# Attention of the samples in a decoder step: keys turned by VectorE in 32x32 blocks, scores in sixteen array tiles, their partial sums added by products with stacked identities

## What is computed

```python
def one(args):
    ql, qp, cn, kn, pages = args
    cp = cache_ckv[pages].reshape(-1, KV_LORA)
    kp = cache_kpe[pages].reshape(-1, QK_ROPE_DIM)
    n_past = cp.shape[0]
    s_past = (jnp.einsum('thl,pl->htp', ql, cp) + jnp.einsum('thr,pr->htp', qp, kp)).astype(jnp.float32) * ATTN_SCALE
    s_new = (jnp.einsum('thl,sl->hts', ql, cn) + jnp.einsum('thr,sr->hts', qp, kn)).astype(jnp.float32) * ATTN_SCALE
    s_new = jnp.where(causal, s_new, -jnp.inf)
    p = jax.nn.softmax(jnp.concatenate([s_past, s_new], axis=-1), axis=-1).astype(cp.dtype)
    return jnp.einsum('htp,pl->thl', p[..., :n_past], cp) + jnp.einsum('hts,sl->thl', p[..., n_past:], cn)
```

## Time and profile before

| | before |
|---|---|
| median of 3 executions | 1428.21 us |
| profiled execution, its own time | 1430.2 us |
| profiled execution, its span | 1428.1 us |
| TensorE (PE) busy | 1373.9 us, 96% |
| VectorE (DVE) busy | 829.4 us, 58% |
| ScalarE (ACT) busy | 612.6 us, 43% |
| GpSimd (POOL) busy | 728.0 us, 51% |
| bytes moved | 148.67 MB, of which the gathers 41.95 MB |

### The profile page before, as it was taken

The page is one execution under the profiler, slowest core; times in us unless marked ns, Lnnn a source line. Parts: engine busy times, 40 slices in busy tenths (PEclk is TensorE's granted clock), DMA queues, the critical chain, the costliest instruction groups (busy, mean ns, idle before and its releaser), DMA issues.

```text
span 1428.1 us, 28640 instructions
## 1 busy us (share of the span) xinstructions
PE 1373.9 (96%) x12250; PEld 1274.6 (89%) x12250; DVE 829.4 (58%) x1247; ACT 612.6 (43%) x1044; POOL 728.0 (51%) x505
## 2 busy tenths in 40 slices
PE   6999989999999999999999988889999999999997
PEld 6778679999999999999999856566999999999997
DVE  6768865755464553767566645555475554645434
ACT  5222354644344343444666533343364443444432
POOL 3333113388788786443323533330346787887831
PEclk9999989999999999999999999999999999999998
DMA  9221202223322224432111576661122223222221
GB/s 226 61 57 35 92 0 90 89 91 103 103 90 89 90 90 139 148 99 65 34 34 53 198 270 252 253 228 41 60 89 89 89 92 112 94 89 89 89 89 63
DMA packets 123181, 148.67 MB, mean 104 GB/s; under 512 B 13552, under 2 KB 114160, under 8 KB 118832
## 3 DMA queue, kind: packets, MB, share of 16 engines
q1 hardware_dynamic: 115888, 104.90, 23.4%
q0 software_dynamic: 7168, 41.95, 7.8%
HBM read 142.81 MB, written 4.03 MB: 103 GB/s over the span
## 4 chain that ended last, share of the span: by engine, by line
PE 93%; DVE 4%; ACT 2%; issue 1%; DMA 0%; POOL 0%; DVEq 0%; SPq 0%; ACTq 0%
PE ps L1609 33%; PE ps L1756 20%; PE ps L1744 18%; PE ps L1888 6%; PE ps L1652 4%; PE ps L1928 3%; PE ps L1980 2%; ACT wh L678 1%; PE ps L1661 1%; PE ps L1673 1%; PE ps L1971 1%; PE ps L1989 0%; PE ps L1713 0%; PE ps L1833 0%; DVE kt L1447 0%
## 5 line engine op out<-in xcount | busy, mean ns | idle before, releaser
L541 POOL TENSOR_TENSOR wl<-raw,wh 128x512 fp32r<-128x512 f32 (+2 forms) x252 | 439.9, 1748 | 443.2 <-ACT wh L678 443.0
L678 ACT ACTIVATE wh<-raw 128x512 fp32r<-128x512 f32 (+2 forms) x253 | 192.6, 762 | 376.1 <-PE ps L1609 205.9
L541 POOL TENSOR_TENSOR wl<-wuv,wh 128x512 fp32r<-128x512 f32 x104 | 135.3, 1312 | 78.1 <-ACT wh L678 78.1
L1609 PE MATMUL ps<-xh,wh 128*128 128x272 f32 x704 | 149.9, 294 | 14.0 <-DVE xl L1033 13.3
L1756 PE MATMUL ps<-mh,wl 128*128 128x272 f32 x768 | 158.6, 288 | 0.0
L1756 PE MATMUL ps<-mh,wh 128*128 128x272 f32 x768 | 158.6, 288 | 0.0
L1756 PE MATMUL ps<-ml,wh 128*128 128x272 f32 x768 | 158.3, 288 | 0.0
L1609 PE MATMUL ps<-xh,wl 128*128 128x272 f32 x704 | 146.3, 290 | 0.0
L1609 PE MATMUL ps<-xl,wh 128*128 128x272 f32 x704 | 146.0, 289 | 0.0
L1609 PEld LDWEIGHTS ps<-xh,wh 128*128 128x128 f32 x704 | 111.4, 191 | 25.2 <-POOL wl L541 11.5
L1756 PEld LDWEIGHTS ps<-ml,wh 128*128 128x128 f32 x768 | 120.4, 188 | 0.0
(11 more groups left out here) (316 smaller groups left out, 3052.7 us busy)
## 6 DMA issues: line engine op xcount, KB each, us to landing
raw<-w_up SPq DMA_DIRECT2D x32, 1024.0 KB, 5.2
raw<-w_down SPq DMA_DIRECT2D x32, 1024.0 KB, 5.0
raw<-w_pw SPq DMA_DIRECT2D x16, 512.0 KB, 5.1
raw<-w_pw SPq DMA_DIRECT2D x4, 1024.0 KB, 6.7
raw<-w_o SPq DMA_DIRECT2D x4, 1024.0 KB, 5.8
raw<-w_dq SPq DMA_DIRECT2D x3, 1024.0 KB, 5.3
raw<-w_uq SPq DMA_DIRECT2D x4, 768.0 KB, 4.4
x<-xT SPq DMA_DIRECT2D x4, 544.0 KB, 7.4
```

Of the source, the lines that this page charges most:

```text
L541: pf.tensor_tensor(weight(wl, u), weight_raw(u), f32(weight(wh, u)), ALU.subtract).then_inc(w_lo, 1)
L678: af.activation(weight(wh, u), weight_raw(u), ACT.Copy).then_inc(w_hi, 1)
L1609: m = tf.matmul(ps[:, bank_of(u) + bank, 0:width], w[:, k, :], a[:, k, part], start=(k == 0 and n == 0), stop=(k == nk - 1 and n == 2))
```

## The change

- VectorE turns the keys itself, from the gathered rows in SBUF to SBUF, with its own transpose (`df.transpose`), which turns each 32x32 block in place: `keys(i, c)` has two transposes of 1024 columns for c = 0 and 1 (the two halves of the latent) into `k_far`, and two of 512 columns for c = 2 (the rotary part) into `k_rot`. The 40 turns on TensorE and the ten copies to `kt` fall away, and `kt` and `ORDER` with them.
- The blocks so turned leave the numbers of one key only in the 32 partitions of its own block. So the scores become products of 32 rows by 32 queries: each of the array's sixteen 32x32 tiles works alone (`scores_s`). The four row tiles r write their own PSUM banks (`RING[r]`), each for the keys whose block lies in these partitions; the four column tiles g hold partial sums over different 32 numbers of the key. For c = 0 and 1 there are 16 products of 512 columns, for c = 2 there are 8.
- ScalarE copies the four banks to `kq` (`quarters_out`), and 16 products of 128 columns with `ident4`, four 32x32 identities stacked on each other, add the four partial sums (`quarters`). They write the bank in which the scores stood before. The columns of the scores now come in another order, which the access pattern of the exponentials and the choice of rows in `values` undo.
- The queries are first brought to the partitions that this needs, once: five pairs of products (`queries_turned`), copied by ScalarE and VectorE into `raw` and `acc`.
- `k_far`, `k_rot` and `kq` have one buffer each. `keys(i + 1, c)` waits until `scores_s(i, c)` is done (`k_used`).
- `kq` and the queries lie in `raw`, so all loads of `w_o` behind the first wait until the last scores are added.
- Copies of outputs and the collecting (`values_out`, `collect`) move from VectorE to ScalarE. `folds` moves to POOL, between gathers, but for the last. `weights` is split in `differences` and `weights`.
- On TensorE the scores for c = 0 and 1 of the next piece stand where the turns stood; those for c = 2 stand before `values`.

The diff, cut to its core:

```diff
         r_in = [sem(f"r_in{i}") for i in range(CB)]
-        kt_mm, kt_act, kt_dve = sem("kt_mm"), sem("kt_act"), sem("kt_dve")
+        q_mm, q_act, q_dve = sem("q_mm"), sem("q_act"), sem("q_dve")
...
         RSTD = ps[:, 4:6, :].rearrange("p a b -> p (a b)")[:, 0:T]
-        def keys_at(n):
-            return ps[:, RING[n % 4], :]
...
+        def q_of(j):
+            return q_near[:, j, :] if j < DC else q_rot[:, j - DC, :]
+
+        def k_of(j):
+            return k_far[:, j // 4, :, SB * (j % 4):SB * (j % 4 + 1)] if j < DC else k_rot[:, :, SB * (j - DC):SB * (j - DC + 1)]
...
             for n in range(units[U_WO].block, len(blocks)):
+                if n == units[U_WO].block + 1:
+                    sp.wait_ge(ks_mm, NSC)
                 load(n)
...
+            def folds(b):
+                pool.wait_ge(e_wn, b + 1)
+                if b >= SETS:
+                    pool.wait_ge(e_mm, 1)
+                for s in range(SETS):
+                    pf.tensor_tensor(fold_w[NS * s:NS * (s + 1), b % SETS, :, :], ident32.unsqueeze(1).to_broadcast([NS, SPB, NS]),
+                                     wn[:, s, :].unsqueeze(2).to_broadcast([NS, SPB, NS]), ALU.mult).then_inc(e_fold, 1)
+                g = b % SETS
+                pf.tensor_scalar(fold_new[NS * g:NS * (g + 1), g, :], ident32, wn[:, SETS, 0:1], None, ALU.mult).then_inc(e_fold, 1)
+
...
             for j in range(4, NCH):
                 gather(j)
+                if j > CB and (j - CB) % (2 * SPB) == 3:
+                    folds((j - CB) // (2 * SPB))
+            folds(NB - 2)
...
+            def queries_turned(p):
+                act.wait_ge(q_mm, p + 1)
+                af.activation(q_pair(p).rearrange("p j q -> p (j q)"), q_bank(p), ACT.Copy).then_inc(q_act, 1)
...
-                    keys(0, (0, 2))
+                    act.wait_ge(w_lo, PROJ[NH - 1] + 1)
+                    queries_turned(0)
+                    queries_turned(2)
...
+            def quarters_out(i):
+                act.wait_ge(k_used, 3 * (i + 1))
+                if i > 0:
+                    act.wait_ge(ks_mm, i)
+                for g in range(GROUPS):
+                    af.activation(kq[:, g, :], ps[:, RING[g], :], ACT.Copy).then_inc(kq_out, 1)
+
+            def values_out(i):
+                act.wait_ge(ko_mm, i + 2)
+                if i >= SETS * SPB:
+                    act.wait_ge(e_mm, 1)
+                af.activation(oc_at(i), ps[:, 6, 0:KL], ACT.Copy).then_inc(ko_out, 1)
...
+            def collect(b):
...
-            keys(0, (8,))
+            act.wait_ge(w_lo, U_WO + 2)
             for i in range(NSC):
-                keys(i + 1, (0,))
+                quarters_out(i)
+                if i == 0:
...
+                if i == FOLD_AT + 1:
+                    turned_out(0)
+                if i > 0 and i != FOLD_AT:
+                    values_out(i - 1)
+                if i % SPB == 0 and i > 0:
+                    weights_out(i // SPB - 1)
                 act.wait_ge(ks_max, i + 1)
-                af.activation(ss[:, :], ps[:, 3 + i % 2, :], ACT.Exp, bias=nmx[:, i % SETS:i % SETS + 1], scale=SCALE,
-                              accum_out=st[:, i % SETS, 1:2]).then_inc(ks_exp, 1)
+                af.activation(ss[:, :].rearrange("p (g i s) -> p i g s", g=SETS, i=GROUPS),
+                              ps[:, 3 + i % 2, :].rearrange("p (i g s) -> p i g s", i=GROUPS, g=SETS), ACT.Exp,
+                              bias=nmx[:, i % SETS:i % SETS + 1], scale=SCALE, accum_out=st[:, i % SETS, 1:2]).then_inc(ks_exp, 1)
                 if i == FOLD_AT:
+                    values_out(i - 1)
                     folded_out(0)
-                keys(i + 1, (2, 4, 6))
+                if i % SPB == SPB - 1:
+                    collect(i // SPB)
                 probs_out(i)
-                if i == FOLD_AT:
-                    turned_out(0)
-                keys(i + 1, (8,))
-                if i % SPB == SPB - 1:
-                    weights_out(i // SPB)
+            weights_out(NB - 1)
+            values_out(NSC - 1)
...
+            def keys(i, c, halves_=(0, 1)):
+
                 if i >= NSC:
                     return
-                for g in groups:
-                    dve.wait_ge(kt_mm, 10 * i + g + 1)
-                    df.tensor_copy(kt[:, ORDER[g], :], keys_at(10 * i + g)).then_inc(kt_dve, 1)
+                if i > 0:
+                    dve.wait_ge(k_used, 3 * (i - 1) + c + 1)
+                for g in halves_:
+                    j = 2 * i + g
+                    if c == 0:
+                        dve.wait_ge(c_in[j % CB], 16 * (j // CB + 1))
+                    if c == 2:
+                        dve.wait_ge(r_in[j % CB], 16 * (j // CB + 1))
+                    to, a = ((k_rot[:, RPC * g:RPC * (g + 1), :], rotaries(j).rearrange("p (r l) -> p r l", r=RPC)) if c == 2 else
+                             (k_far[:, c, RPC * g:RPC * (g + 1), :],
+                              latents(j).rearrange("p (r l) -> p r l", r=RPC)[:, :, c * P:(c + 1) * P]))
+                    df.transpose(to, a).then_inc(k_turned, 1)
...
-            def collect(b):
...
-            def weights(b):
+            def differences(b):
...
+            def weights(b):
...
-            keys(0, (3, 5, 7, 9))
+            keys(0, 0, (1,))
+            queries_turned(3)
+            keys(0, 1)
+            keys(0, 2)
             for i in range(NSC):
-                if i > 0 and i != FOLD_AT:
-                    values_out(i - 1)
+                keys(i + 1, 0)
+                keys(i + 1, 1)
+                if i % SPB == 0 and i > 0:
+                    weights(i // SPB - 1)
                 dve.wait_ge(ks_mm, i + 1)
                 m = st[:, i % SETS, 0:1]
                 link(df.tensor_reduce(m, ps[:, 3 + i % 2, :], AX.X, ALU.max))
                 df.tensor_scalar(nmx[:, i % SETS:i % SETS + 1], m, -SCALE, None, ALU.mult).then_inc(ks_max, 1)
-                if i == 0:
-                    dve.wait_ge(ko_mm, 1)
-                    df.tensor_copy(onew[:, :, :].rearrange("p a b -> p (a b)"), ps[:, 6, :]).then_inc(ko_out, 1)
-                if i == FOLD_AT:
-                    values_out(i - 1)
-                keys(i + 1, (1, 3, 5, 7, 9))
+                keys(i + 1, 2)
                 if i % SPB == SPB - 1:
-                    collect(i // SPB)
-                    weights(i // SPB)
-                elif i > 0:
-                    folds(i // SPB - 1)
+                    differences(i // SPB)
+            weights(NB - 1)
             folds(NB - 1)
-            values_out(NSC - 1)
...
-            def keys(i, groups):
...
-                    for q in range(4):
-                        a = (rotaries(j)[:, 2 * q * ROPE:2 * (q + 1) * ROPE] if k == 4 else
-                             latents(j)[:, (2 * q + k // 2) * KL + (k % 2) * P:(2 * q + k // 2) * KL + (k % 2 + 1) * P])
-                        m = tf.transpose(keys_at(n)[:, q * P:(q + 1) * P], a, ident)
-                    m.then_inc(kt_mm, 1)
+            def queries_turned(p):
+
+                for n in range(2):
+                    j = 2 * p + n
+                    row = SB * (j % 4)
+                    for r in range(GROUPS):
+                        m = tf.matmul(q_bank(p)[SB * r:SB * (r + 1), n * NB * NS:(n + 1) * NB * NS], ident[:, row:row + SB],
+                                      qs[:, j // 4, :, :].rearrange("p b q -> p (b q)"), start=True, stop=True)
+                m.then_inc(q_mm, 1)
...
@@ -1915,19 +1964,31 @@
                     if h // 2 + 1 < NH // 2:
                         values_product(h // 2 + 1, h % 2)
                 else:
-                    keys(0, range(3))
+                    pe.wait_ge(kcopy, 2 + 4 * NH // 2 + KC)
+                    for p in range(3):
+                        queries_turned(p)
                 outputs(h)
 
             def scores_s(i, c):
+
                 b = i // SPB
-                pe.wait_ge(kt_act, 5 * i + (4, 5, 5)[c])
-                pe.wait_ge(kt_dve, 5 * i + (3, 4, 5)[c])
-                for s in range(SETS):
-                    q = qs[:, c if c < KC else KC + s % 2, b, :]
-                    k = kt[:, 5 * (s // 2) + (2 * (s % 2) + c if c < KC else 4), :]
-                    m = tf.matmul(ps[NS * s:NS * (s + 1), 3 + i % 2, :], q, k, start=(c == 0), stop=(c == 2))
-                if c == 2:
-                    m.then_inc(ks_mm, 1)
+                pe.wait_ge(k_turned, 6 * i + 2 * c + 2)
+                for r in range(GROUPS):
+                    part = slice(SB * r, SB * (r + 1))
+                    for g in range(GROUPS if c < 2 else 2):
+                        j = 4 * c + g
+                        m = tf.matmul(ps[SB * g:SB * (g + 1), RING[r], :], q_of(j)[part, b * NS:(b + 1) * NS], k_of(j)[part, :, :],
+                                      start=(c == 0), stop=(c == (2 if g < 2 else 1)))
+                m.then_inc(k_used, 1)
+
+            def quarters(i):
+
+                for r in range(GROUPS):
```

(39 more changed lines are left out.)

69 lines of the change are left out of this document (31 added, 38 removed).

## The result

The changed kernel is slower, by 1.9%: 1457.95 us median of 4 (1453.6 to 1459.61), beside 1429.2 (1428.06 to 1432.48) of the kernel before; ratio 1.0193, 95% interval 1.0164 to 1.0221. The forecast was 1387 us. The profiled execution took 1453.6 us, with a span of 1451.8. The first maximum of the loop starts at 833.77 us (forecast 828.0), the last at 1012.38 (947.0): the loop takes 178.6 us instead of 119.0, and this is where nearly all of the miss lies. Behind it nothing changed (439.4 us of span against 440.7 before).

What follows compares the result with a forecast made beforehand. VectorE was to bound the changed loop at 8.05 us a piece instead of 10.95; -40.4 us to the last maximum and -0.6 behind took 1430.2 to 1389.2 profiled, the median 2.0 lower: 1387 us, range 1380 to 1396.

Steps and rivals of the forecast that it cites:

- the price of the scores: TensorE in each piece: 80 score instructions at 34 ns, the convolution's pace, 2.7 us.
- The gathers: Cache loads per piece: POOL issues in 5.0 us, data take 6.9 us, fitting in 8.05 with slack 1.5.
- the head: Before the loop: the first maximum waits for VectorE alone and starts at 828.0 us instead of 825.0.
- the sum: VectorE's work per piece in the loop: 0.98 + 6.14 + 0.93 = 8.05 us, where a piece took 10.95.
- rival 1: Loop: gathers or TensorE bound it, VectorE being quicker; 7.3 us a piece, 1376 us; chance 0.12.
- The gain: Whole program: -40.4 us to the last maximum and -0.6 behind it, -41.0 from the profiled 1430.2.
- Transposes: VectorE's turning of keys: 1.20 us for 1024 columns and 0.67 for 512, near a copy's pace.
- Rival 3: VectorE's transposes run at half the copy's pace, 13.0 us a piece; slower kernel, 1465 us; chance 0.13.
- The c = 2 scores: TensorE's rotary-part scores in each piece, counted among the 80 score instructions at 34 ns each.
- The identities: TensorE adding partial sums in each piece: 32 instructions of 128 columns, 1.1 to 1.9 us, taken at 1.1.
- Rival 4: Loop: TensorE's clock falls to 0.50 through idling, 11.5 us a piece, 1438 us; chance 0.05.
- The w_o loads: After the last scores: each lands in 5.8 us, hidden by the first two units; zero cost, otherwise 6.

Runs made afterwards that it cites:

- e8: Changed kernel with the scores' two loops exchanged, so each column group's four row groups follow each other: 1391.1 us, 0.9878 of the kernel before.
- e4b: Changed kernel with chunks 7 to 31 loaded by plain SyncE transfers of consecutive rows, run where the unaltered changed kernel took 1453.3 us: 1391.0 us.
- e3: Changed kernel with as many gathers, but those of chunks 7 to 31 landing 0.5 MB a chunk in place of 1.25: 1379.8 us.
- e2: Kernel before the change with only the first seven of 32 cache chunks gathered, the rest read from what buffers hold: 1410.3 us, ratio 1.0002.
- e4: Changed kernel with chunks 7 to 31 loaded by plain SyncE transfers of consecutive rows in place of POOL's gathers: 1385.1 us, 0.9833 of the kernel before.
- e1: Changed kernel with only the first seven of 32 cache chunks gathered, later ones worked on from what buffers hold: 1380.3 us, 0.9792 of the kernel before.
- e7: Changed kernel with each pair of gathers issued only after the next piece's c = 0 and 1 scores: 1439.6 us, 1.0212 of the kernel before.

## Why the prediction was wrong

- **The failed step is the price of the scores: "80 x 0.034 = 2.7 us".** The row it came from, the convolution's, holds for TensorE without gathers beside it. The gathers were costed by their landing and by POOL's time; that their issuing could cost TensorE something was in no term. On the chip of the result 64 of the 80 instructions take 7.3 us (877.01 to 884.35), 16 more 1.89, and the fourteen pieces that were put at 8.05 us take 12.3 in the mean (833.77 to 1006.18), most of them 10 to 14.5. With the head (833.77 for 828.0), the loop (178.6 for 119.0) and a tail 0.7 shorter than forecast, that makes 5.8 + 59.6 - 0.7 = 64.7 us; the profiled execution is 64.4 over the 1389.2 that were forecast for it.
- **Without the disturbance the sum holds.** e8 has a loop of 120.6 us (828.91 to 949.54) and e4b, on a disturbed chip but without POOL's gathers, 118.1, beside 119.0. That is partly luck. VectorE was quicker than counted: with small data (e3) the pieces are 6.5 us, and 8.4 with a sample's weights, where 7.1 and 9.0 were counted, and the loop takes 110.8. In e8 the landing of the data takes up the difference, a limit that the sum had as slack and rival 1 had as the bound.
- **The gain was counted against a disturbed measure.** 1428 us held 19 us that a quiet chip doesn't take (1409.4 there, with or without the gathers). Of its piece of 10.95 us, 9.39 stay in e2. That the 19 are the same disturbance is likely but not shown: the kernel before never ran without gathers on a disturbed chip. On a quiet chip the change brings some 20 us, not 41, by e4 and e8.
- **A sign of it stood in the earlier trace rows**: the first maximum began after 4.20 us of idling, ended by "remote" (2.05 in e2). The scores that it waits for are in the timeline of the kernel before, which I hadn't set beside it:

```profile
820.02 2.78 PE L1928 MATMUL ps<-kt,qs 128*32 128x512 f32 x24
```

They end at 822.80 and the maximum starts 2.2 us later, at 825.01. In e2 the same products end at 819.09 and the maximum starts at 819.16:

```profile
816.31 2.78 PE L1929 MATMUL ps<-kt,qs 128*32 128x512 f32 x24
```

```profile
819.16 0.69 DVE L1543 TENSOR_REDUCE st<-ps 128x1 f32<-128x512 f32 x1 [2.05 <-PE ps L1929]
```

- **Transposes: right.** 1.211 and 0.690 us, taken at 1.20 and 0.67. Rival 3, which held 0.13 of the 0.18 given to a slower kernel, was wrong: the kernel is slower for another reason.
- **The c = 2 scores were mis-sized.** 16 instructions were counted at 34 ns, 0.54 us; they take 1.09 at full clock (e3), nearly as long as 32 that use all sixteen tiles (1.15 in e1); half the tiles stand empty. On VectorE's loop it cost nothing. The identities were right: 1.06 us for 32.
- **Rival 4, the clock, came true in part, for another reason.** On the chip of the result it fell to 1.2 GHz in ten of the first fourteen pieces, in the slow stretch and not through idling behind VectorE. Such idling left it at 1.00 in the loops of e1 and e3; it fell once in e4b's (at 864.9 us), and often in e7's, where data came late. Its 1438 us had the pieces at 11.5 us, near the measured 12.3, and a chance of 0.05.
- **The head** was 5.8 us late. R(0) lies between 823.9 and 830.5 us on quiet chips and between 830.8 and 835.5 on disturbed ones, with 828.0 forecast. The first chunks' gathers disturb it as well: 32 score instructions beside them take 5.66 us (from 823.14, most of it at 1.2 GHz), in e8 1.15.
- POOL issues the four gathers in 4.7 us (843.85 to 848.56), not in 5.0 as the prediction read; this changed nothing.
- The w_o loads, POOL's folds (0.35 us each) and the collecting cost nothing on the path, as taken.
